# Gathering token rows with one float32 one-hot matmul instead of three bf16 ones, in a two-layer MoE trunk

## The chip, the cores and the metric

The kernel runs on one core of one Trainium2 chip. The metric is the time on the device of one execution, in microseconds (us). Three runs of the kernel before took 1240.8, 1241.95 and 1242.02 us, so the median is 1241.95 us. Lower is better.

## The reference, cut to what matters

Two layers work on 256 tokens (`S`) of width 1024 (`D`), all in float32. Each layer is a token mixer with a LayerNorm, and then a mixture of 64 experts with a LayerNorm. The part around the change is the mixture:

```python
top_idx, top_w = route(xf, w_router, router_bias)   # 8 of 64 experts per token
y = routed_experts(xf, top_idx, top_w, ...) + swiglu(xf, ws_gate, ws_up, ws_down)
# routed_experts: rows xf[tok] are gathered by expert, then
#   h = silu(x @ w_gate[e]) * (x @ w_up[e]);  yb = h @ w_down[e]       (width 256)
# and yb * weight is summed back into each token's row
```

## The kernel before, in words

**Everything on one core.** The residual stream `xs` lies in SBUF as two tiles of 128 tokens by 1024 (f32). Each layer has a prologue (projections, attention, LayerNorm, router, shared expert; some 150 us) and then the routed experts: 32 pairs of experts, one after the other. `SLOTS` is 32, so each expert takes at most 32 tokens per pass. A pair is therefore 64 columns, and a block of two pairs is 128. If an expert has more tokens, further rounds run through a branch; they are not run for these inputs.

**One pair on TensorE** is `body` in the second `run`, L583 to L627. The order of its work is written out by hand:

1. gate and up, L596: 32 f32 matmuls of 64 by 512, half of them in each 64-column half of the array, from `xg` (the gathered tokens, transposed) and the pair's weights `GU`;
2. a quarter of the gather for the next block, `gather`, L511 to L520: 12 matmuls into PSUM bank `G`, only in pairs 0 to 29;
3. `combine` of the pair before (L542);
4. two transposes of the hidden activations (L608), after `h_rd`;
5. another quarter of the gather, only in pairs 0 to 29;
6. down, L622: 64 matmuls, after `hT_sb`;
7. `turn_sel` for the next pair, L522 to L534, in pairs 0 to 30: the one-hot matrix is transposed and the routing weights are gathered into slots.

**The gather.** `sel` is the one-hot matrix (token by slot) that VectorE builds at L1146. `xsp` holds x as three bf16 parts, `hi`, `mid` and `lo`. For each of the 8 slices of 128 features and both token tiles, three matmuls with stationary `xsp[:, t, s, k::KD]` and moving `sel` accumulate in PSUM. ScalarE copies each full bank of G to `xg` (`g_quarter`, L925, recorded at L912). The two blocks take turns on `xT` and `xg_odd`. The first block of a layer is gathered in one go before pair 0: 48 matmuls into four banks, followed by four copies on ScalarE; the gate of pair 0 waits for the last copy (`g_sb`).

**What the parts cost elsewhere.** ScalarE makes `hi` and `mid` (`split`, L1025), VectorE makes the remainder and `lo` (L1109, L1113), and `weights` (L1115 to L1129) splits the routing weights the same way into `w3`. `take_selT` (L1150) copies the transposed one-hot matrix out of G and adds three parts of a weight (L1156).

**The weights' loads.** SyncE (SP) issues every DMA, all on one queue. There are three weight slots in SBUF. SP's `body` (L428) waits until the gate of pair n-3 is done (`h_full`), issues the 4 MB gate and up load of pair n (L411), waits for the down product of pair n-3 (`y_full`) and issues the 2 MB down load of pair n (L414). TensorE waits for `w_in[0]` before the gate and for `w_in[1]` before the down product. Pairs 0 and 1 are loaded during the prologue; that of pair 2 is issued when `sh1` and `acc3` are full, near the prologue's end, and that of pair 3 when the gate of pair 0 is done. After the last pair of the first layer, the attention loads of the next layer follow in the same queue.

In step 2 and step 5 the calls are:

```python
if filling:
    if j == 0:
        pe.wait_ge(ps.sel_rd, first_block + B + 2)
    pe.wait_ge(ps.selT_sb, n + 1)
    gather(ps, first_block + B + 1, 2 * j, (B + 1) % 2)
...
if filling:
    pe.wait_ge(ps.g_sb, fills + 1)
    gather(ps, first_block + B + 1, 2 * j + 1, (B + 1) % 2)
```

Of the kernel before, what the change touches and what calls it, by code (L numbers as in the profile page):

```python
# [25 lines left out]
P = 128  # L26
# [15 lines left out]
SMALL_W = KD * E + E + 2 * HD + 2  # L42
SCRATCH = 9920
BLOCKS = PAIRS // 2
# [98 lines left out]
def build(nc, x, xt, memt, dense, shared_dn, small_w, ln1_g, ln1_b, w_gu, w_dn, ln2_g, ln2_b,  # L143
          consts, before_ones, pool_mat, out):
    with ExitStack() as ctx:
        def sb(name, shape, dt=F32):
            return ctx.enter_context(nc.sbuf_tensor(name, shape, dt))

        def sem(name):
            return ctx.enter_context(nc.semaphore(name))  # L150
# [11 lines left out]
        small = sb("small", [P, 76])  # L162
        identb = sb("identb", [P, P], BF16)
        bo = sb("bo", [P, P])
# [5 lines left out]
        def part(n, dt=F32):  # L170

            v = scratch[:, off[0]:off[0] + n]
            off[0] += n
            assert off[0] <= SCRATCH, off[0]
            return v if dt == F32 else v.bitcast(dt)
# [20 lines left out]
        off[0] = 0  # L196
        xsp = part(NT * 3 * D // 2, BF16).rearrange("p (t s d) -> p t s d", t=NT, s=3)
        xres = part(NT * D).rearrange("p (t d) -> p t d", t=NT)
        yres = xres[:, 0, :]
        off[0] -= D  # L200
        xg_odd = part(KD * 2 * P)
# [3 lines left out]
        sg = part(2 * F).rearrange("p (t n) -> p t n", t=NT)  # L205
        sel = part(2 * NT * P // 2, BF16).rearrange("p (b t c) -> p b t c", b=2, t=NT)
        selT = part(2 * P // 2, BF16).rearrange("p (b s) -> p b s", b=2)
        pos = part(NT * E)
        w3 = part(NT * E * 3 // 2, BF16).rearrange("p (t e s) -> p t e s", t=NT, s=3)

        off[0] = NT * 3 * D // 2 + D + KD * 2 * P
        sig = part(NT * E)
        biased = part(NT * E)
        masked = part(NT * E)
        chosen = part(NT * E)
        wts = part(NT * E)
        wres = part(NT * E)
        chosenb = part(NT * E // 2, BF16)
# [6 lines left out]
        top = part(NT * 8)  # L225
        assert off[0] <= NT * 3 * D // 2 + D + KD * 2 * P + 3 * D // 2
        counts_i = sb("counts_i", [P, 1], I32)
# [16 lines left out]
        def cc(name):  # L244
            return cst[:, CONSTS[name][0]:CONSTS[name][1]]
# [23 lines left out]
        x_in = sem("x_in")  # L269
        setup_done = sem("setup_done")  # L270
        small_in = sem("small_in")
# [15 lines left out]
        route_rd = sem("route_rd")  # L287
        w3_rd = sem("w3_rd")
        split_hi = sem("split_hi")
        split_rs = sem("split_rs")  # L290
        split_rd = sem("split_rd")
        ssilu = sem("ssilu")
# [35 lines left out]
        def x_at(l, i, t):  # L328

            return x_ready, 4 * l + 2 * i + t + 2  # L330
# [166 lines left out]
        def _(pe):  # L497
# [13 lines left out]
            def gather(ps, B, quarter, buf, to=G):  # L511

                for kk in range(2):
                    k = 2 * quarter + kk
                    for t in range(NT):
                        for s in range(3):
                            m = pe.matmul(to[:].rearrange("p (k x t c) -> p k x t c", k=2, x=4, t=NT)[:, kk, :, t, :],  # L517
                                          xsp[:, t, s, k::KD], sel[:, buf, t, :].rearrange("p (x c) -> p x c", x=4),
                                          start=s == 0, stop=s == 2)
                m.then_inc(ps.g_full, 1)  # L520

            def turn_sel(ps, q):  # L522

                if ps is not main:
                    stand_alone(pe)
                gb = G[:].bitcast(BF16)
                half = sel[:, q // 2 % 2, :, 64 * (q % 2):64 * (q % 2) + 64]
                for t in range(NT):
                    pe.transpose(gb[64 * t:64 * t + 64, 0:P], half[:, t, :], identb[:])  # L529
                for t in range(NT):  # L530
                    wq = w3[:, t].rearrange("p (r e) s -> p r (e s)", e=2)
                    m = pe.matmul(G[64 * t:64 * t + 64, 256:262], half[:, t, :], wq[:, q, :],
                                  start=True, stop=True)
                m.then_inc(ps.selT_ps, 1)  # L534
# [36 lines left out]
            def run(ps, l, turn, round_):  # L571
# [7 lines left out]
                if round_ is None:  # L579
                    pe.wait_ge(w3_rd, l + 1)  # L580
                turn_sel(ps, 0)
# [55 lines left out]
            for l in range(DEPTH):  # L637
# [172 lines left out]
                if l == 0:  # L810
                    pe.wait_ge(setup_done, 1)
                turn_probs(0)
# [89 lines left out]
                shared_down(l)  # L902
                pe.wait_ge(split_rd, 2 * l + 2)
                run(main, l, l, None)
# [4 lines left out]
        def _(act):  # L909

            def copy(out_, in_, **kw):
                return act.activation(out_, in_, ACT.Copy, **kw)  # L912
# [44 lines left out]
            for l in range(DEPTH):  # L957
# [66 lines left out]

                def split(t, part):  # L1025

                    if part == 0:
                        act.wait_ge(*x_at(l, 0, t))
                        copy(xsp[:, t, 0, :], xs[:, t, :]).then_inc(split_hi, 1)
                    else:  # L1030
                        act.wait_ge(split_rs, 2 * l + t + 1)
                        copy(xsp[:, t, 1, :], xres[:, t, :]).then_inc(split_hi, 1)

                def turned_tile(t):
# [13 lines left out]
                turned_tile(0)  # L1048
                split(0, 0)
                exp_logits(0)  # L1050
                turned_tile(1)
                split(1, 0)
                exp_logits(1)
                prepare(ACT.Silu)
                split(0, 1)
                shared_silu(0)
                shared_silu(1)
                evac(l, "shT", hT)
                split(1, 1)
                run(main, l, l, None)  # L1060
# [4 lines left out]
        def _(dve):  # L1065
            dve.memset(small[:], 0.0)
            dve.memset(power[:], -0.5).then_inc(power_set, 1)
            for s_ in [*read, x_ready]:
                dve.sem_inc(s_, 1)
            dve.wait_ge(const_in, 32)  # L1070
            dve.tensor_copy(identb[:], ident).then_inc(setup_done, 1)
            links = [0]
# [33 lines left out]

            def split_residual(l, t):
                dve.wait_ge(split_hi, 4 * l + t + 1)
                dve.tensor_tensor(xres[:, t, :], xs[:, t, :], xsp[:, t, 0, :], ALU.subtract).then_inc(split_rs, 1)  # L1109

            def split_last(l, t):
                dve.wait_ge(split_hi, 4 * l + 2 + t + 1)
                dve.tensor_tensor(xsp[:, t, 2, :], xres[:, t, :], xsp[:, t, 1, :], ALU.subtract).then_inc(split_rd, 1)  # L1113

            def weights(l, t):  # L1115

                def tile(v, n=E):
                    return v[:, t * n:(t + 1) * n]
                chosen_, sig_, wts_, wres_ = map(tile, (chosen, sig, wts, wres))
                link(dve.tensor_tensor_reduce(wts_, chosen_, sig_, 1.0, 0.0, ALU.mult, ALU.add, wsum[:, t:t + 1]))  # L1120
                link(dve.reciprocal(wrec[:, t:t + 1], wsum[:, t:t + 1]))
                link(dve.tensor_scalar(wts_, wts_, wrec[:, t:t + 1], ROUTED_SCALE, ALU.mult, ALU.mult))
                part3 = [w3[:, t, :, s_] for s_ in range(3)]
                link(dve.tensor_copy(part3[0], wts_))
                link(dve.tensor_tensor(wres_, wts_, part3[0], ALU.subtract))
                link(dve.tensor_copy(part3[1], wres_))
                m = dve.tensor_tensor(part3[2], wres_, part3[1], ALU.subtract)
                if t == NT - 1:
                    m.then_inc(w3_rd, 1)  # L1129

# [4 lines left out]
            def run(ps, l, turn, round_):  # L1135
# [14 lines left out]
                def take_selT(n, b):  # L1150
                    dve.wait_ge(ps.selT_ps, n + 1)
                    dve.tensor_copy(selT[:, b, :], G[:].bitcast(BF16)[:, 0:P])
                    for t in range(NT):
                        for e in range(2):
                            r0 = 64 * t + 32 * e
                            m = dve.tensor_reduce(wslot[r0:r0 + 32, b:b + 1], G[r0:r0 + 32, 256 + 3 * e:259 + 3 * e],  # L1156
                                                  AX.X, ALU.add)
                    m.then_inc(ps.selT_sb, 1)
                build_sel(0)
                if round_ is None:  # L1160
                    split_residual(l, 1)
                    split_last(l, 0)
                    split_last(l, 1)
                    weights(l, 0)
                    weights(l, 1)
                    count_slots(l)
# [38 lines left out]
            for l in range(DEPTH):  # L1205
                begin(dve, l, within)
                if l:
# [3 lines left out]
                                    take(l, "xTa3")[:, :].rearrange("p (k s) -> p k s", k=4)).then_inc(read[BANK_OF["xTa3"]], 1)  # L1211

                cos2 = cc("cos").unsqueeze(1).to_broadcast([P, 2, S])
                sin2 = cc("sin").unsqueeze(1).to_broadcast([P, 2, S])
# [70 lines left out]
                normalised(l, 0, 0)  # L1285
                split_residual(l, 0)

# [113 lines left out]
```

## Time and profile before

| | |
|---|---|
| median of 3 runs | 1241.95 us |
| the profiled execution's own time | 1242.17 us |
| its span, first to last instruction | 1240.2 us |
| mean granted TensorE clock | 0.995 of full speed |
| TensorE matmul busy | 1199.5 us (97% of the span) |
| TensorE weight loads busy | 550.5 us (44%) |
| VectorE / ScalarE busy | 426.9 us / 335.4 us |
| read from HBM | 450.15 MB |

How to read it: PE is TensorE's matmuls, PEld its weight loads (they overlap PE), DVE is VectorE, ACT is ScalarE, SPq is the queue of SyncE, L517 is line 517 of the kernel. Matmuls are pipelined, so the duration of one is longer than the distance between two, and a busy PE is not PE at its peak. The span is about 2 us shorter than the execution's own time. "Landing" is the time from the issue of a DMA to its completion.

### The profile page before, as it was taken

To read this page: it belongs to the slowest core of one execution; us is meant where nothing else is said; L and a number is where in the kernel's file an instruction comes from. 1 tells how busy PE (TensorE), PEld (TensorE's weight loads), DVE (VectorE), ACT (ScalarE), POOL (GpSimd) and SP (SyncE) were. 2 spreads that over 40 slices of the span, in tenths; PEclk is the share of its full clock that TensorE was granted. 3 is DMA by queue.
4 is the path that set the end of the run, shared out by engine and by line. 5 is a ranking of instruction groups with operands and counts; after the bars stand their busy time and mean duration, and the time that the engine had idled before them with its cause. 6 is when DMAs were issued, how large, how long until landed. Compare 5 with 4: busy or idle time off the path is not lost.

```text
span 1240.2 us, 18632 instructions
## 1 busy us (share of the span) xinstructions
PE 1199.5 (97%) x8032; PEld 550.5 (44%) x8032; DVE 426.9 (34%) x1198; ACT 335.4 (27%) x637; POOL 10.4 (1%) x20
## 2 busy tenths in 40 slices
PE   7999899999999999999899999999999999999994
PEld 5764443333443334433386645344333443334431
DVE  0433732332333323333334336233333333333335
ACT  0132222322223222233212323222232222322221
POOL 0000000000000000000010000000000000000001
PEclk9999999999999999999999999999999999999998
DMA  9962389999999999999967405899999999999990
GB/s 390 417 282 80 103 358 435 424 435 425 432 424 427 429 432 429 432 426 433 423 248 309 193 35 221 362 429 430 430 433 427 431 429 428 429 429 428 429 400 37
DMA packets 26713, 452.48 MB, mean 365 GB/s; under 512 B 2944, under 2 KB 3072, under 8 KB 5504
## 3 DMA queue, kind: packets, MB, share of 16 engines
q1 hardware_dynamic: 26624, 451.21, 86.1%
q8 instruction: 66, 1.08, 0.4%
q14 instruction: 23, 0.19, 0.0%
HBM read 450.15 MB, written 1.05 MB: 364 GB/s over the span
## 4 chain that ended last, share of the span: by engine, by line
PE 95%; DVE 3%; DMA 1%; ACT 1%; issue 0%; POOL 0%; SPq 0%; POOLq 0%
PE bank L596 36%; PE bank L622 18%; PE bank L517 8%; PE bank L542 7%; PE bank L678 4%; PE bank L750 4%; PE bank L687 2%; PE bank L608 2%; PE bank L877 1%; PE bank L697 1%; PE bank L566 1%; PE bank L707 1%; PE bank L652 1%; PE bank L646 1%; PE bank L529 1%; DMA slots<-in_dense 1%
## 5 line engine op out<-in xcount | busy, mean ns | idle before, releaser
L622 PE MATMUL bank<-slots,scratch 128*32 128x512 f32 x2048 | 233.0, 595 | 2.3 <-issue 2.3
L596 PE MATMUL bank<-slots,xT 128*64 128x512 f32 x1024 | 226.1, 594 | 1.0 <-ACT xT L912 1.0
L596 PE MATMUL bank<-slots,scratch 128*64 128x512 f32 x1024 | 226.0, 594 | 0.0
L1183 DVE SCALAR_TENSOR_TENSOR scratch<-bank,small,scratch 128x512 f32<-128x512 f32 x128 | 96.1, 751 | 248.7 <-ACT scratch L912 248.7
L912 ACT ACTIVATE scratch<-bank,small 128x512 bf16<-128x512 f32 x128 | 87.9, 687 | 159.0 <-PE bank L622 159.0
L912 ACT ACTIVATE scratch<-bank 128x512 f32<-128x512 f32 (+2 forms) x122 | 67.0, 562 | 236.0 <-PE bank L517 76.9
L517 PEld LDWEIGHTS bank<-scratch 128*128 128x128 bf16 x1536 | 107.7, 146 | 50.4 <-issue 49.7
L596 PEld LDWEIGHTS bank<-slots,xT 128*64 128x64 f32 x1024 | 69.3, 137 | 130.6 <-issue 129.3
L596 PEld LDWEIGHTS bank<-slots,scratch 128*64 128x64 f32 x1024 | 69.2, 137 | 129.4 <-issue 129.4
L517 PE MATMUL bank<-scratch 128*128 128x128 bf16 x1536 | 117.1, 227 | 0.3
L622 PEld LDWEIGHTS bank<-slots,scratch 128*32 128x32 f32 x2048 | 60.8, 109 | 121.1 <-issue 117.1
L1175 DVE TENSOR_TENSOR scratch<-scratch,bank 128x256 f32<-128x256 f32 x64 | 26.9, 421 | 250.0 <-ACT scratch L934 250.0
L934 ACT ACTIVATE scratch<-bank 128x256 f32<-128x256 f32 x64 | 24.6, 384 | 321.2 <-PE bank L596 321.2
L542 PE MATMUL bank<-scratch 64*128 64x512 bf16 x768 | 94.5, 379 | 5.9 <-DVE scratch L1190 5.9
L912 ACT ACTIVATE scratch<-scratch 128x512 bf16<-128x512 f32 (+1 forms) x132 | 84.2, 638 | 21.5 <-DVE scratch L1183 19.2
L1190 DVE TENSOR_TENSOR scratch<-scratch 128x512 bf16<-128x512 f32 x128 | 82.9, 688 | 2.1
L912 ACT ACTIVATE xT<-bank 128x512 f32<-128x512 f32 x75 | 44.1, 597 | 115.2 <-PE bank L517 80.4
L1177 DVE COPY scratch<-bank 128x256 f32<-128x256 f32 x64 | 27.2, 424 | 113.6 <-PE bank L608 113.6
L750 PE MATMUL bank<-slots,scratch 128*128 128x512 f32 x128 | 58.2, 600 | 0.0
L678 PE MATMUL bank<-xT,slots 128*128 128x256 f32 x256 | 55.7, 379 | 1.1 <-DVE xT L1210 1.1
L542 PEld LDWEIGHTS bank<-scratch 64*128 64x128 bf16 x768 | 32.3, 94 | 45.2 <-DVE scratch L1190 7.8
L678 PEld LDWEIGHTS bank<-xT,slots 128*128 128x128 f32 x256 | 48.6, 190 | 7.8 <-issue 1.3
(125 smaller groups left out, 697.2 us busy)
## 6 DMA issues: line engine op xcount, KB each, us to landing
slots<-in_w_gu SPq DMA_DIRECT2D x64, 4096.0 KB, 22.6
slots<-in_w_dn SPq DMA_DIRECT2D x64, 2048.0 KB, 20.9
slots<-in_dense SPq DMA_DIRECT2D x32, 1024.0 KB, 11.3
r<-in_pool_mat SPq DMA_DIRECT2D x2, 1024.0 KB, 19.7
r<-in_ln_g SPq DMA_DIRECT2D x4, 512.0 KB, 4.5
r<-in_ln_b SPq DMA_DIRECT2D x4, 512.0 KB, 5.9
slots<-in_shared_dn SPq DMA_DIRECT2D x2, 1024.0 KB, 4.9
scratch<-in_memt SPq DMA_DIRECT2D x2, 512.0 KB, 6.8
```

The lines of the kernel that those rows point to most:

```text
L517: m = pe.matmul(to[:].rearrange("p (k x t c) -> p k x t c", k=2, x=4, t=NT)[:, kk, :, t, :], xsp[:, t, s, k::KD], sel[:, buf, t, :].rearra ...
L542: m = pe.matmul(acc[2 * t + half][:, :], selT[64 * t:64 * t + 64, b, :], ysp[64 * t:64 * t + 64, s, half * 512:(half + 1) * 512], start=Fa ...
L596: m = pe.matmul(H[64 * a:64 * a + 64, :], xg[B % 2][:, k, j, a, :], GU[g][:, a, :, k, :], start=k == 0, stop=k == KD - 1)
L608: m = pe.transpose(H[:, kc * P:(kc + 1) * P], hh[:, 0, kc::KF], ident)
L622: m = pe.matmul(Y[half][r0:r0 + 32, :], hT[:, kc * P + 64 * a + 32 * t:kc * P + 64 * a + 32 * t + 32], DN[g][:, a, kc, half * 512:(half + ...
L678: m = pe.matmul(o[:, j * S:(j + 1) * S], W[c][:, k, (2 * (i % 2) + j) * P:(2 * (i % 2) + j + 1) * P], xT[:, k, :], start=k == 0, stop=k == ...
L750: m = pe.matmul(o[:, :], mixT[:, k, t * P:(t + 1) * P], w[:, k, :], start=first, stop=k == KD - 1, skip_group_check=True)
L912: return act.activation(out_, in_, ACT.Copy, **kw)
L1175: dve.tensor_tensor(hh[:, 0, :], sg[:, 0, :], H[:, F:2 * F], ALU.mult).then_inc(ps.h_rd, 1)
L1177: dve.tensor_copy(hT[:, 0:F], H[:, 0:F]).then_inc(ps.hT_sb, 1)
L1183: dve.scalar_tensor_tensor(yres[:, half * 512:(half + 1) * 512], Y[half][:, :], wslot[:, b:b + 1], ysp[:, 0, half * 512:(half + 1) * 512], ...
L1190: dve.tensor_tensor(ysp[:, 2, half * 512:(half + 1) * 512], yres[:, half * 512:(half + 1) * 512], ysp[:, 1, half * 512:(half + 1) * 512], ...
```

## The change

The gather takes f32 `xs` itself as the stationary operand and an f32 `sel` as the moving one, with one matmul where there were three. In `turn_sel` the bf16 transposes become f32 matmuls against the identity, and the routing weights are gathered straight from f32 `wts`, two columns for each tile. The four instructions of `turn_sel` are now ordered by tile. `xsp`, `xres`, `w3`, `identb`, all splits (ScalarE's two copies and VectorE's two subtractions per tile and layer, four instructions per tile in `weights`) and their semaphores go. The scratch is laid out anew, with `yres` and `sel` in places of their own.

```diff
             def gather(ps, B, quarter, buf, to=G):
                 for kk in range(2):
                     k = 2 * quarter + kk
                     for t in range(NT):
-                        for s in range(3):
-                            m = pe.matmul(to[:].rearrange("p (k x t c) -> p k x t c", k=2, x=4, t=NT)[:, kk, :, t, :],
-                                          xsp[:, t, s, k::KD], sel[:, buf, t, :].rearrange("p (x c) -> p x c", x=4),
-                                          start=s == 0, stop=s == 2)
+                        m = pe.matmul(to[:].rearrange("p (k x t c) -> p k x t c", k=2, x=4, t=NT)[:, kk, :, t, :],
+                                      xs[:, t, k::KD], sel[:, buf, t, :].rearrange("p (x c) -> p x c", x=4),
+                                      start=True, stop=True)
                 m.then_inc(ps.g_full, 1)
             def turn_sel(ps, q):
-                gb = G[:].bitcast(BF16)
                 half = sel[:, q // 2 % 2, :, 64 * (q % 2):64 * (q % 2) + 64]
                 for t in range(NT):
-                    pe.transpose(gb[64 * t:64 * t + 64, 0:P], half[:, t, :], identb[:])
-                for t in range(NT):
-                    wq = w3[:, t].rearrange("p (r e) s -> p r (e s)", e=2)
-                    m = pe.matmul(G[64 * t:64 * t + 64, 256:262], half[:, t, :], wq[:, q, :],
+                    pe.matmul(G[64 * t:64 * t + 64, 0:P], half[:, t, :], ident, start=True, stop=True)
+                    m = pe.matmul(G[64 * t:64 * t + 64, 256:258], half[:, t, :], wts[:, t * E + 2 * q:t * E + 2 * q + 2],
                                   start=True, stop=True)
...
                 if round_ is None:
-                    pe.wait_ge(w3_rd, l + 1)
+                    pe.wait_ge(weights_rd, l + 1)
...
                 shared_down(l)
-                pe.wait_ge(split_rd, 2 * l + 2)
                 run(main, l, l, None)
...
                 turned_tile(0)
-                split(0, 0)
                 exp_logits(0)
                 turned_tile(1)
-                split(1, 0)
                 exp_logits(1)
                 prepare(ACT.Silu)
-                split(0, 1)
                 shared_silu(0)
                 shared_silu(1)
                 evac(l, "shT", hT)
-                split(1, 1)
                 run(main, l, l, None)
...
                 def take_selT(n, b):
                     dve.wait_ge(ps.selT_ps, n + 1)
-                    dve.tensor_copy(selT[:, b, :], G[:].bitcast(BF16)[:, 0:P])
+                    dve.tensor_copy(selT[:, b, :], G[:, 0:P])
                     for t in range(NT):
                         for e in range(2):
                             r0 = 64 * t + 32 * e
-                            m = dve.tensor_reduce(wslot[r0:r0 + 32, b:b + 1], G[r0:r0 + 32, 256 + 3 * e:259 + 3 * e],
-                                                  AX.X, ALU.add)
+                            m = dve.tensor_copy(wslot[r0:r0 + 32, b:b + 1], G[r0:r0 + 32, 256 + e:257 + e])
                     m.then_inc(ps.selT_sb, 1)
                 build_sel(0)
                 if round_ is None:
-                    split_residual(l, 1)
-                    split_last(l, 0)
-                    split_last(l, 1)
                     weights(l, 0)
```

## Rows read from the trace of the kernel before

**Rows 1.** The page: engines (1), slices of 31 us (2), chain that ended last (4).
```profile
PE 1199.5 (97%) x8032; PEld 550.5 (44%) x8032; DVE 426.9 (34%) x1198; ACT 335.4 (27%) x637; POOL 10.4 (1%) x20
DMA  9962389999999999999967405899999999999990
PE 95%; DVE 3%; DMA 1%; ACT 1%; issue 0%; POOL 0%; SPq 0%; POOLq 0%
```
**Rows 2.** Timeline of one pair: start, length, engine, line, what [idle before].
```profile
500.92 7.06 PE L596 MATMUL bank<-slots,xT 128*64 128x512 f32 x32
507.91 0.95 PE L517 MATMUL bank<-scratch 128*128 128x128 bf16 x12
508.79 1.47 PE L542 MATMUL bank<-scratch 64*128 64x512 bf16 x12
510.19 0.51 PE L608 MATMUL bank<-cst,scratch 128*128 128x128 f32 x2
510.54 0.90 PE L517 MATMUL bank<-scratch 128*128 128x128 bf16 x12
510.74 0.42 DVE L1177 COPY scratch<-bank 128x256 f32<-128x256 f32 x1 [1.87 <-PE bank L608]
511.36 3.64 PE L622 MATMUL bank<-slots,scratch 128*32 128x512 f32 x32
514.93 0.25 PE L529 MATMUL bank<-identb,scratch 128*64 128x128 bf16 x2
515.04 7.06 PE L596 MATMUL bank<-slots,xT 128*64 128x512 f32 x32
```
**Rows 3.** DMA view, loads issued at 169.90, 183.11, 564.53, 1174.40 us, in that order.
```profile
slots<-in_w_gu SPq DMA_DIRECT2D x1, 4096.0 KB, 13.9
...
slots<-in_w_gu SPq DMA_DIRECT2D x1, 4096.0 KB, 15.1
...
slots<-in_w_gu SPq DMA_DIRECT2D x1, 4096.0 KB, 32.6
...
slots<-in_w_gu SPq DMA_DIRECT2D x1, 4096.0 KB, 32.3
```
**Rows 4.** Two stretches: us, busy by engine, PEclk, DMA share, GB/s.
```profile
183.00:597.00 414.00, 413.44 (x3110) 164.19 (x3112) 131.36 (x349) 119.31 (x204) 0.00 (x0) 1.00 1.00 429
168.00:170.00 2.00, 2.00 (x13) 0.62 (x10) 0.00 (x0) 0.10 (x1) 0.00 (x0) 1.00 0.00 0
```
**Rows 5.** Timeline of TensorE, the gates of pair 31 in both layers.
```profile
598.82 7.06 PE L596 MATMUL bank<-slots,scratch 128*64 128x512 f32 x32
...
1208.69 7.06 PE L596 MATMUL bank<-slots,scratch 128*64 128x512 f32 x32
```
**Rows 6.** Timeline of TensorE in the prologues, f32 matmuls of other widths.
```profile
25.05 21.32 PE L678 MATMUL bank<-xT,slots 128*128 128x256 f32 x98
...
138.33 1.16 PE L859 MATMUL bank<-cst,xs 128*128 128x128 f32 x8 [0.68 <-DVE xs L1105]
...
73.78 0.87 PE L795 MATMUL bank<-scratch 128*64 128x256 f32 x8
```
**Rows 7.** Timeline of the first layer before pair 0, and a pair of copies earlier.
```profile
158.95 3.13 PE L517 MATMUL bank<-scratch 128*128 128x128 bf16 x48
159.90 2.82 ACT L912 ACTIVATE xT<-bank 128x512 f32<-128x512 f32 x4 [5.75 <-PE bank L517]
...
162.77 7.09 PE L596 MATMUL bank<-slots,xT 128*64 128x512 f32 x32 [0.51 <-ACT xT L912]
...
139.08 1.08 ACT L912 ACTIVATE xT<-bank 128x512 f32<-128x512 f32 x2 [8.09 <-PE bank L859]
```
**Rows 8.** Timeline of pair 30, which has no gather.
```profile
594.07 0.50 PE L608 MATMUL bank<-cst,scratch 128*128 128x128 f32 x2
594.61 0.42 DVE L1177 COPY scratch<-bank 128x256 f32<-128x256 f32 x1 [0.98 <-PE bank L608]
595.14 3.64 PE L622 MATMUL bank<-slots,scratch 128*32 128x512 f32 x32 [0.56 <-issue]
```

More of the change, by code:

```diff
@@ L42 @@
 SMALL_W = KD * E + E + 2 * HD + 2
-SCRATCH = 9920
+SCRATCH = 9728
 BLOCKS = PAIRS // 2
@@ L162, in build @@
         small = sb("small", [P, 76])
-        identb = sb("identb", [P, P], BF16)
         bo = sb("bo", [P, P])
@@ L196, in build @@
         off[0] = 0
[L197 to L200, printed above, removed]
+        yres = part(D)
+        sel = part(2 * NT * P).rearrange("p (b t c) -> p b t c", b=2, t=NT)
+        off[0] += 4 * D - D - 2 * NT * P
         xg_odd = part(KD * 2 * P)
@@ L205, in build @@
         sg = part(2 * F).rearrange("p (t n) -> p t n", t=NT)
-        sel = part(2 * NT * P // 2, BF16).rearrange("p (b t c) -> p b t c", b=2, t=NT)
         selT = part(2 * P // 2, BF16).rearrange("p (b s) -> p b s", b=2)
         pos = part(NT * E)
-        w3 = part(NT * E * 3 // 2, BF16).rearrange("p (t e s) -> p t e s", t=NT, s=3)
-        off[0] = NT * 3 * D // 2 + D + KD * 2 * P
+        wts = part(NT * E)
+        off[0] = 4 * D + KD * 2 * P
         sig = part(NT * E)
@@ L215, in build @@
         chosen = part(NT * E)
-        wts = part(NT * E)
-        wres = part(NT * E)
         chosenb = part(NT * E // 2, BF16)
@@ L225, in build @@
         top = part(NT * 8)
-        assert off[0] <= NT * 3 * D // 2 + D + KD * 2 * P + 3 * D // 2
+        assert off[0] <= 4 * D + KD * 2 * P + 3 * D // 2
         counts_i = sb("counts_i", [P, 1], I32)
@@ L269, in build @@
         x_in = sem("x_in")
-        setup_done = sem("setup_done")
         small_in = sem("small_in")
@@ L287, in build @@
         route_rd = sem("route_rd")
[L288 to L291, printed above, removed]
+        weights_rd = sem("weights_rd")
         ssilu = sem("ssilu")
@@ L810, in _ @@
                 if l == 0:
-                    pe.wait_ge(setup_done, 1)
+                    pe.wait_ge(const_in, 32)
                 turn_probs(0)
@@ L1023, in _ @@
                 heads_out(5)
[L1025 to L1032, printed above, removed]
                 def turned_tile(t):
@@ L1069, in _ @@
                 dve.sem_inc(s_, 1)
-            dve.wait_ge(const_in, 32)
-            dve.tensor_copy(identb[:], ident).then_inc(setup_done, 1)
             links = [0]
@@ L1105, in normalised @@
                 dve.scalar_tensor_tensor(v, v, rstd[:, t:t + 1], lnb, ALU.mult, ALU.add).then_inc(x_ready, 1)
[L1107 to L1113, printed above, removed]
             def weights(l, t):
@@ L1118, in tile @@
                     return v[:, t * n:(t + 1) * n]
-                chosen_, sig_, wts_, wres_ = map(tile, (chosen, sig, wts, wres))
+                chosen_, sig_, wts_ = map(tile, (chosen, sig, wts))
                 link(dve.tensor_tensor_reduce(wts_, chosen_, sig_, 1.0, 0.0, ALU.mult, ALU.add, wsum[:, t:t + 1]))
                 link(dve.reciprocal(wrec[:, t:t + 1], wsum[:, t:t + 1]))
[L1122 to L1127, printed above, removed]
+                m = dve.tensor_scalar(wts_, wts_, wrec[:, t:t + 1], ROUTED_SCALE, ALU.mult, ALU.mult)
                 if t == NT - 1:
-                    m.then_inc(w3_rd, 1)
+                    m.then_inc(weights_rd, 1)
             def count_slots(l):
@@ L1211, in _ @@
                                     take(l, "xTa3")[:, :].rearrange("p (k s) -> p k s", k=4)).then_inc(read[BANK_OF["xTa3"]], 1)
+                if l == 0:
+                    dve.wait_ge(const_in, 32)
                 cos2 = cc("cos").unsqueeze(1).to_broadcast([P, 2, S])
@@ L1285, in _ @@
                 normalised(l, 0, 0)
-                split_residual(l, 0)
                 def choose(t):
```

## The prediction

> **What bounds the kernel now.** I read the page first: the chain that ended last is TensorE for 95%, and its matmuls are busy 97% of the span [rows 1]. That alone would make TensorE the bound and every TensorE saving a gain. The DMA row of the slices says otherwise: through both expert stages it stands at 9 in nearly every slice too [rows 1], and the view of stretches gives a DMA share of 1.00 at 429 GB/s from 183 to 597 us [rows 4]. So two resources are full, and the question is which has the slack.
>
> The timeline of one pair gives TensorE's pace: gate to gate 515.04 - 500.92 = 14.12 us, without a gap [rows 2]. The landings give the DMA's. Pair 3's gate load is issued at 169.90 and takes 13.9, so it lands at 183.8; pair 31's is issued at 564.53 and takes 32.6, so it lands at 597.1 [rows 3]. That is 413.3 us for 28 loads, 14.76 us per pair. The DMA is slower than TensorE; each load lands a little later against its issue (15.1 us for pair 4, 32.6 for pair 31), and the stage ends before the head start of three slots is used up. How near it comes: the gate of pair 31 starts at 598.82 [rows 5], 1.7 us after its weights have landed; in the second layer at 1208.69 [rows 5] against 1174.40 + 32.3 = 1206.7 [rows 3], 2.0 us. TensorE is the bound by these 2 us per layer and no more.
>
> **The change, part by part.**
>
> The gather in a pair. Now 12 bf16 matmuls take 507.91 to 508.79 = 0.88 us until the combine starts [rows 2]. Afterwards there are 4 f32 matmuls of 128 columns. No such gather is in the trace; the nearest rows are 98 f32 matmuls of 256 columns in 21.32 us, 0.218 each [rows 6], half of which is 0.11, and eight f32 transposes in 1.16 us [rows 6], 0.14 each with the start and the tail of the group, whose stationary operand is `xs` with the same stride of 8. I take 0.11 each and 0.20 for start and handing over, 0.65 us (0.55 to 0.70). **The first quarter saves 0.23 us** (0.18 to 0.33).
>
> The second quarter lies beside a wait. The down product needs VectorE's copy of the transposed activations: copy at 510.74 for 0.42, down at 511.36 [rows 2]. In pair 30, with no gather between, transposes to down still takes 595.14 - 594.07 = 1.07 us, with the copy [rows 8], against 1.17 with it (511.36 - 510.19, [rows 2]). So **the second quarter saves at most 0.10 us**, I take 0.09: what is late next is the copy. The bounds are 0 and 0.10.
>
> `turn_sel`. Now all four of its instructions hold the next gate up by 515.04 - 514.93 = 0.11 us [rows 2], because they are bf16 and the two column halves overlap. Afterwards each tile has an f32 matmul of 128 columns and one of 2 columns in the same half behind it; ordered by tile, the second tile starts after the first's narrow one. The nearest row is eight f32 matmuls with 64-wide weights in 0.87 us [rows 6], four of them 256 columns wide. I take 0.11 for each tile and 0.08 around, 0.30 us, **0.19 more than now** (0.05 to 0.45 more).
>
> Over one layer 30 pairs have gathers and 31 `turn_sel` calls lie between the gates of pair 0 and pair 31: TensorE's own path gets 30 x 0.32 - 31 x 0.19 = 3.7 us shorter.
>
> The first block of a layer. 48 matmuls take 3.13 us, ScalarE's four copies 2.82 us, and the gate starts at 162.77 after the last copy [rows 7]. With 16 matmuls at 0.11, a bank is full every 0.45 us and the copies become the limit. Two copies in a row take 1.08 us [rows 7], one 0.60, so the step is 0.48 and four take 2.04. A bf16 matmul costs 3.13 / 48 = 0.065 [rows 7], so the first bank is full 0.3 us earlier (12 x 0.065 against 4 x 0.11). Copies from 159.60 to 161.64: **the gate of pair 0 starts 1.1 us earlier** (0.7 to 1.2). The f32 `turn_sel` lies inside that wait.
>
> The splits and the four instructions for `w3`: nothing. VectorE and ScalarE do them under the shared expert's down product and under the shared expert's matmuls; none stands in the chain before the gather, which follows the down product directly. With them gone, that cover hides nothing. `sel` in f32, the copy of `selT` from an f32 bank and four copies for four reductions lie beside a gate of 7.06 us [rows 2]: nothing, and some tenths of a us on VectorE if that cover went. No DMA is added or removed; SP's queue is the same.
>
> What the DMA does with it. Pair 3's load waits for the gate of pair 0, and the DMA is idle then (0 GB/s from 168 to 170 us, [rows 4]), so it moves 1.1 us forward with the gate. After that the queue is never empty and a slot freed earlier only waits longer in it. Pair 31's weights land at 597.1 - 1.1 = 596.0, in the second layer 1206.7 - 1.1 = 1205.6 before the first layer's own gain. TensorE would be ready for them 1.1 + 3.7 = 4.8 us earlier than now, at 594.0. **So it waits there for the load**, some 2 us, and of 4.8 us only 1.7 + 1.1 = 2.8 remain, less 0.1 from landing to first matmul: 2.7 in the first layer, 2.0 + 1.1 - 0.1 = 3.0 in the second.
>
> **The sum:** 1242.17 - 2.7 - 3.0 = 1236.5 us for the profiled execution, which was 0.2 above the median of the runs; for the median 1236.3 us.
>
> Two rules of the Trainium skill bear on this. The landings show a DMA that moves 429 GB/s and not more while it is full [rows 4]. The page "DMA: Bandwidth & Descriptors", section "Where 436 GB/s comes from", puts the ceiling at 435.2 GB/s; a pair's 6.29 MB (4096 + 2048 KB) would take 14.5 us by it, an estimate from that page, which is still slower than TensorE, so the floor would stand. The other rule speaks against the change: f32 at 256 columns costs 0.218 us here [rows 6], two columns' time for each column. "FP8 and Floating Point Precision", section "TensorE Precision Notes", says that true FP32 takes four passes through the array; then four f32 matmuls would cost more than twelve bf16 ones. By that rule, the trace does not agree: it shows half that price.
>
> **The rivals.**
>
> *The DMA gives way (10%).* If the landings could come faster once slots are free earlier, TensorE's whole 4.8 us per layer would count: 1242.0 - 9.6 = 1232.3 us, and with the best bounds of the terms still less. For it: TensorE is the chain's 95%. Against it: a share of 1.00 over 414 us, and landings that fall ever further behind.
>
> *`turn_sel` eats the gather (9%; the other side).* The f32 pieces in `turn_sel` stand open on the path in 31 of 32 pairs. At its upper bound of 0.45 more, with the first quarter at 0.18, TensorE's path grows by 31 x 0.45 - 30 x 0.27 = 5.9 us, less 1.1 at the layer's start: 4.8 us slower per layer, 1251.5 us; at 0.40 and 0.27 it is 1248.5. It decides from 31 x turn - 30 x gather > 1.1 on. Against it: two f32 pieces of 0.11 don't reach 0.4 us.
>
> *Double price per f32 column (2%; the other side).* At 0.22 us for 128 f32 columns, the gather quarter would take 1.07 us instead of 0.88, and the second quarter would outlast its copy. With `turn_sel` at 0.4 more, a pair costs about 0.8 us more and the kernel about 1242 + 2 x (31 x 0.8 - 1) = 1290 us. The row of 256 columns in 0.218 us [rows 6] speaks against it. The rule of four passes, named above, would lead here.
>
> *No change (13%).* The DMA's margin of 2 us could be smaller than it looks, for instance if a wait of 2 us before pair 31 is followed by a stretch of TensorE at 1.2 GHz, or if the loads take 0.3% longer in other runs (1.3 us per layer). Then 1240 to 1243.
>
> **How the numbers follow.** A change under 0.2% (2.5 us) can't be told from none here. The forecast of 1236.3 holds 66%; by its bounds (start 0.7 to 1.2 us, a DMA pace 0.2% off either way) its own range is 1234 to 1239.5. To hold 8 of 10, the range reaches down over most of the first rival and up to no change: 1231.5 to 1242.0. Faster by over 0.2%: the forecast and the first rival, 0.76. Same: no change, 0.13. Slower: the two on the other side, 0.11.
>
> **What the profile afterwards would show.** Right: L517 with 512 f32 matmuls in place of 1536, 0.6 to 0.7 us from gather to combine; the down product 1.1 us after the transposes; about 0.3 us between down and the next gate; the gate of pair 0 of the first layer at 161.7; DMA share 1.00; pair pace near 14.0 us and, in the last one or two pairs, a wait of L596 on DMA of up to 3 us, which doesn't stand in the trace now. Wrong: no wait on DMA at all and the landings closer to their issues (first rival); a pair pace over 14.12 (the other side); an end near 1242 with waits on DMA all over.

## The result: 14% slower, and the profile after

The changed kernel took 1410.8 us (median of 4 runs, 1410.5 to 1411.4) against 1242.0 us before (4 runs of the same comparison). The ratio is 1.136, with a 95% interval of 1.135 to 1.138: 168.8 us slower.

| | before | after |
|---|---|---|
| the profiled execution | 1242.17 us | 1410.57 us |
| its span | 1240.2 us | 1408.7 us |
| PE / PEld busy | 1199.5 / 550.5 us | 1368.4 / 720.7 us |
| DVE / ACT busy | 426.9 / 335.4 us | 417.5 / 327.7 us |
| one pair, gate to gate | 14.12 us | 16.75 us |

The page of the changed kernel: engines, DMA in slices, the chain, and from part 5 the gather's two groups.

```profile
PE 1368.4 (97%) x7776; PEld 720.7 (51%) x7776; DVE 417.5 (30%) x1173; ACT 327.7 (23%) x629; POOL 10.4 (1%) x20
DMA  9941599999999999999747227999999999999930
PE 95%; DVE 2%; DMA 1%; ACT 1%; issue 0%; POOL 0%; SPq 0%; POOLq 0%
L507 PEld LDWEIGHTS bank<-scratch,xs 128*128 128x128 f32 x1024 | 253.0, 332 | 50.7 <-issue 49.2
L507 PE MATMUL bank<-scratch,xs 128*128 128x128 f32 x1024 | 269.0, 407 | 0.9 <-ACT scratch L898 0.9
```

Two things stand in the gather's lines at once. The count is 1024, where I had said 512: the program has 512 f32 matmuls (4 in each quarter), and the profile has two instructions for each. And a weight load takes 332 ns, where the f32 weight loads of the projections take 190. TensorE remains the bound by the same shares as before [rows 1]; the shares say nothing of why it takes longer.

One pair of the changed kernel, TensorE and the copy that the down product waits for (start, length, engine, line, what). It answers to [rows 2]:

```profile
501.34 7.07 PE L583 MATMUL bank<-slots,xT 128*64 128x512 f32 x32
508.34 2.17 PE L507 MATMUL bank<-scratch,xs 128*128 128x128 f32 x8
510.44 1.47 PE L529 MATMUL bank<-scratch 64*128 64x512 bf16 x12
511.84 0.50 PE L595 MATMUL bank<-cst,scratch 128*128 128x128 f32 x2
512.18 2.05 PE L507 MATMUL bank<-scratch,xs 128*128 128x128 f32 x8
512.39 0.42 DVE L1131 COPY scratch<-bank 128x256 f32<-128x256 f32 x1 [3.09 <-PE bank L595]
514.16 3.64 PE L609 MATMUL bank<-slots,scratch 128*32 128x512 f32 x32
517.74 0.45 PE L518 MATMUL bank<-cst,scratch 128*64 128x128 f32 x4
518.09 7.07 PE L583 MATMUL bank<-slots,xT 128*64 128x512 f32 x32
```

The whole difference can be read here. First quarter: 508.34 to 510.44 = 2.10 us for 0.88, so 1.22 more. From transposes to down: 514.16 - 511.84 = 2.32 for 1.17, so 1.15 more; the copy at 512.39 has long been done, and the gather itself now holds up the down product. `turn_sel` to gate: 0.35 for 0.11, so 0.24 more. Together 2.61 us per pair. The pace gives 16.75 - 14.12 = 2.63. Thirty pairs in each of two layers make 158 us.

The start of a layer, which answers to [rows 7] (the first and last copies of four are shown):

```profile
158.72 7.65 PE L507 MATMUL bank<-scratch,xs 128*128 128x128 f32 x32
160.69 0.60 ACT L898 ACTIVATE xT<-bank 128x512 f32<-128x512 f32 x1 [8.99 <-PE bank L507]
...
166.40 0.60 ACT L898 ACTIVATE xT<-bank 128x512 f32<-128x512 f32 x1 [1.31 <-PE bank L507]
167.05 7.09 PE L583 MATMUL bank<-slots,xT 128*64 128x512 f32 x32 [0.25 <-ACT xT L898]
```

The gate of pair 0 starts at 167.05, not at 162.77 [rows 7]: 4.3 us later. In the second layer its distance from the gate of pair 31 before it is 178.4 us for 173.8, 4.5 more; together 8.8. ScalarE's copies wait 1.3 us each for the gather, so they never became the limit. Adding up, 158 + 8.8 + 0.5 (two last calls of `turn_sel`) = 167.3 of the 168.5 us between the spans. The rest stands in the last combine:

```profile
1392.01 2.74 PE L529 MATMUL bank<-scratch 64*128 64x512 bf16 x12 [2.97 <-DVE scratch L1144]
```

It took 2.74 us at a granted clock of 0.50, the level of 1.2 GHz. In the trace of before, the same group, after a wait just as long (2.97 us), took 1.47 us at a clock of 1.00. Nothing in the traces ties this 1.3 us to the change.

### The profile page after: what moved, and what is told of

It is laid out like the page before. It is cut to its first block, busy times and chain, and to the rows that moved or that the text cites. A ratio compares the mean times of both kernels' runs of the same rounds, so it can differ in the third digit from the quotient of the medians.

```text
span 1408.7 us, 18086 instructions
## 1 busy us (share of the span) xinstructions
PE 1368.4 (97%) x7776; PEld 720.7 (51%) x7776; DVE 417.5 (30%) x1173; ACT 327.7 (23%) x629; POOL 10.4 (1%) x20
## 4 chain that ended last, share of the span: by engine, by line
PE 95%; DVE 2%; DMA 1%; ACT 1%; issue 0%; POOL 0%; SPq 0%; POOLq 0%
PE bank L583 31%; PE bank L507 18%; PE bank L609 16%; PE bank L529 7%; PE bank L665 4%; PE bank L737 3%; PE bank L674 2%; PE bank L595 2%; PE bank L518 2%; PE bank L864 1%; PE bank L684 1%; PE bank L553 1%; PE bank L694 1%; PE bank L639 1%; PE bank L633 1%; PE bank L770 1%
## 5 line engine op out<-in xcount | busy, mean ns | idle before, releaser
L507 PEld LDWEIGHTS bank<-scratch,xs 128*128 128x128 f32 x1024 | 253.0, 332 | 50.7 <-issue 49.2
L507 PE MATMUL bank<-scratch,xs 128*128 128x128 f32 x1024 | 269.0, 407 | 0.9 <-ACT scratch L898 0.9
L583 PEld LDWEIGHTS bank<-slots,xT 128*64 128x64 f32 x1024 | 73.8, 137 | 125.8 <-issue 125.1
L583 PEld LDWEIGHTS bank<-slots,scratch 128*64 128x64 f32 x1024 | 74.1, 137 | 124.9 <-issue 124.9
L898 ACT ACTIVATE scratch<-scratch 128x512 bf16<-128x512 f32 x128 | 80.0, 625 | 19.3 <-DVE scratch L1137 19.3
```

What stands on the lines that cost most here:

```text
L583: m = pe.matmul(H[64 * a:64 * a + 64, :], xg[B % 2][:, k, j, a, :], GU[g][:, a, :, k, :], start=k == 0, stop=k == KD - 1)
```

## The experiments

Two facts had to be told apart, the number of passes and the price of one; and the prediction's other half, the floor set by the weights' landings, had not been tested at all, since the changed kernel never came near it.

### The stationary operand's stride: 1, 2, 4 against 8 elements

In each of these three kernels ScalarE copies x once per layer, in the prologue, into `xp`, and the f32 gather takes its stationary operand from there. The result is the same, only the distance between neighbouring stationary elements differs. The lines of the contiguous one, without its semaphore and waits; in the others the 1 is a 2 or a 4:

```diff
+        xp = part(NT * D).rearrange("p (t d) -> p t d", t=NT)
...
-                                      xs[:, t, k::KD], sel[:, buf, t, :].rearrange("p (x c) -> p x c", x=4),
+                                      xp[:, t, k // 1 * 1 * P + k % 1:(k // 1 + 1) * 1 * P:1], sel[:, buf, t, :].rearrange("p (x c) -> p x c", x=4),
...
+                    copy(xp[:, t, :].rearrange("p (g q s) -> p g q s", g=KD // 1, s=1),
+                         xs[:, t, :].rearrange("p (q g s) -> p g q s", g=KD // 1, s=1)).then_inc(xp_rd, 1)
```

Contiguous:

> The changed kernel, but x is copied once per layer into contiguous slices of 128 features, and the f32 gather takes its stationary operand from there. The gather is still 8 f32 instructions per quarter. Theory A (the stationary operand's stride of 32 bytes doubles each weight load): weight loads of the gather fall from 332 ns to about 190, matmuls start 0.11 us apart instead of 0.24, a quarter takes 1.1 us instead of 2.1, a pair 14.75 us instead of 16.75, the kernel about 1285 us. Theory B (an f32 matmul of 128 by 128 costs 0.24 us however its operand lies, because of what f32 adds to a load): no change, about 1410 us. Rival C (the PSUM pattern of the output is what slows it): no change either, 1410 us.

Stride 2:

> As the contiguous copy, but neighbouring stationary elements lie 8 bytes apart (stride 2 in f32). Theory A1 (any stride costs the doubling): weight loads of 332 ns, about 1410 us. Theory A2 (two elements out of each 16 bytes are enough, as the skill's page on cachelines has it): about 190 ns and 1285 us. Theory B: 1410 us.

Stride 4:

> As the contiguous copy, but with stride 4 in f32, 16 bytes apart, one element out of each 16 bytes. Theories A1 and A2 and B: 332 ns and 1410 us. Only if the penalty grows with the distance beyond 16 bytes would it lie between 1285 and 1410 us.

| stride, bytes | weight load, mean | kernel | ratio to before |
|---|---|---|---|
| 4 (contiguous) | 192 ns | 1280.0 us (2 runs) | 1.030 [1.028, 1.032] |
| 8 | 197 ns | 1287.4 us (2 runs) | 1.036 [1.034, 1.038] |
| 16 | 327 ns | 1404.8 us (one run) | 1.131 (one run) |
| 32 (the change) | 332 ns | 1410.8 us (4 runs) | 1.136 [1.135, 1.138] |

The gather's groups by line in the contiguous copy, in the stride of 8 bytes and in that of 16 (busy us, mean ns):

```profile
L509 PEld LDWEIGHTS bank<-scratch 128*128 128x128 f32 x1024 | 124.3, 192 | 50.7 <-issue 49.6 <-ACT scratch L901 1.0
```
```profile
L509 PEld LDWEIGHTS bank<-scratch 128*128 128x128 f32 x1024 | 130.7, 197 | 50.8 <-issue 49.6 <-ACT scratch L901 1.1
```
```profile
L509 PEld LDWEIGHTS bank<-scratch 128*128 128x128 f32 x1024 | 248.4, 327 | 50.7 <-issue 49.2 <-ACT scratch L901 1.3
```

And a pair of the contiguous one:

```profile
508.58 1.16 PE L509 MATMUL bank<-scratch 128*128 128x128 f32 x8
509.67 1.47 PE L531 MATMUL bank<-scratch 64*128 64x512 bf16 x12
511.07 0.50 PE L597 MATMUL bank<-cst,scratch 128*128 128x128 f32 x2
511.41 1.06 PE L509 MATMUL bank<-scratch 128*128 128x128 f32 x8
512.40 3.64 PE L611 MATMUL bank<-slots,scratch 128*32 128x512 f32 x32
```

The quarter falls from 2.10 us to 1.09 (508.58 to 509.67), as theory A had it. B (f32 itself) and C (the output's pattern, which is the same in all four) fall. So does A1: at 8 bytes the load is almost as fast as contiguous, at 16 bytes it is slow, and at 32 hardly slower. That the operand is now in `xp` does not explain it either, since the kernel with 16 bytes reads `xp` too and is slow. The step lies between 8 and 16 bytes, that is between two f32 elements out of 16 bytes and one. The Trainium skill's page "Advanced Engine Details and Errata", section "SBUF Cachelines", describes SBUF as having cachelines of 16 bytes and says that at least two hits on one are needed to absorb the access latency. By that rule, these runs agree. They can't tell it from a rule that goes by the distance alone.

### Load or matmul: half of the moving columns

```diff
-                        m = pe.matmul(to[:]...[:, kk, :, t, :],
+                        m = pe.matmul(to[:]...[:, kk, 0:2, t, :],
-                                      xs[:, t, k::KD], sel[:, buf, t, :].rearrange("p (x c) -> p x c", x=4),
+                                      xs[:, t, k::KD], sel[:, buf, t, :].rearrange("p (x c) -> p x c", x=4)[:, 0:2, :],
```

> The changed kernel with the gather's moving operand cut to 64 of its 128 columns (half of the slots are not gathered). Theory L (the strided weight load is the bound and the matmul hides beside it): the step between matmuls stays 0.24 us and the kernel 1410 us. Theory S (with the stride, load and matmul stand one after the other): the step falls by the time of 64 columns, 0.055 us, to 0.18; a pair is 16 x 0.055 = 0.9 us shorter, the kernel 1355 us. If the matmul itself were slow for its output pattern, the step would halve to 0.12 us and the kernel take 1290.

Half of the slots are not gathered, so this kernel's outputs are wrong and only its times are of use. Measured: 1408.9 us (one run), 1.9 us under the changed kernel. A quarter's gather:

```profile
508.98 1.98 PEld L507 LDWEIGHTS bank<-scratch,xs 128*128 128x128 f32 x8 [0.81 <-issue]
508.98 2.11 PE L507 MATMUL bank<-scratch,xs 128*128 128x64 f32 x8
```

The eight loads still take 1.98 us. In the changed kernel they took 1.98 too. Halving the matmuls' columns changed almost nothing (the group takes 2.11 us for 2.17): the strided load sets the step of 0.24 us, and the matmul hides beside it (theory L).

### `turn_sel` alone in f32

The gather stays as before; VectorE builds a second, f32 one-hot `sel32`, and `wts` has a place of its own.

```diff
-                    pe.transpose(gb[64 * t:64 * t + 64, 0:P], half[:, t, :], identb[:])
-                ...
-                    m = pe.matmul(G[64 * t:64 * t + 64, 256:262], half[:, t, :], wq[:, q, :],
+                    pe.matmul(G[64 * t:64 * t + 64, 0:P], half[:, t, :], ident, start=True, stop=True)
+                    m = pe.matmul(G[64 * t:64 * t + 64, 256:258], half[:, t, :], wts[:, t * E + 2 * q:t * E + 2 * q + 2],
                                   start=True, stop=True)
```

> The kernel before with the gather as it was (three bf16 parts, bf16 one-hot) and only turn_sel in f32, from a second one-hot in f32. Theory A: turn_sel on the path goes from 0.11 to 0.36 us, 0.25 us more for each of 62 calls between gates, 1242 + 15.5 = 1257.5 us. Rival D (what grew in the pair is all in the gather, and turn_sel overlaps the next gate): 1242 us. Rival E (f32 turn_sel costs the 0.19 us of the prediction): 1253.8 us.

Measured: 1260.4 us (median of 4), ratio 1.014 [1.012, 1.016], 18 us more. From one pair to the next in its timeline (other lines left out):

```profile
502.44 0.98 PE L519 MATMUL bank<-scratch 128*128 128x128 bf16 x12
503.36 1.47 PE L541 MATMUL bank<-scratch 64*128 64x512 bf16 x12
509.50 0.45 PE L530 MATMUL bank<-cst,sel 128*64 128x128 f32 x4
509.85 7.07 PE L595 MATMUL bank<-slots,xT 128*64 128x512 f32 x32
516.86 0.98 PE L519 MATMUL bank<-scratch 128*128 128x128 bf16 x12
```

`turn_sel` to gate is 509.85 - 509.50 = 0.35 us, 0.24 more than before. The pair takes 516.86 - 502.44 = 14.42 us, 0.30 more. Of the remaining 0.06 us, 0.04 lies between the first gather and the combine (503.36 - 502.44 = 0.92 for 0.88); why is not shown. Rival D (it overlaps) falls. Theory A gave 15.5 us for the measured 18, rival E 11.8.

**The parts add up.** In medians: `turn_sel` in f32 costs 1260.4 - 1242.1 = 18 us; the f32 gather with a contiguous operand a further 1280.0 - 1260.4 = 20 us, which is what two f32 instructions with 128 columns cost beyond three bf16 ones; the stride of 32 bytes 1410.8 - 1280.0 = 131 us. The stride is nearly four fifths of the loss. Even with a contiguous operand, the f32 gather and `turn_sel` cost 38 us more than the bf16 parts.

### The floor of the landings: fewer bf16 parts

To find out what a faster TensorE would have gained, the gather of the kernel before was cut to one part (x rounded to bf16 for the experts) and to two (x rounded to some 16 bits).

```diff
-                        for s in range(3):
+                        for s in range(1):      (range(2) in the other)
-                                          start=s == 0, stop=s == 2)
+                                          start=s == 0, stop=s == 0)      (stop=s == 1)
```

With two parts, the third is not made (`split_last` is gone), and TensorE waits for `split_hi` in place of `split_rd`.

> The kernel before with only the first bf16 part of x gathered: 4 matmuls per quarter instead of 12 (x is then rounded to bf16 for the experts; the other two parts are made but not gathered). It takes 0.48 us from the first quarter and 0.10 from the second, so TensorE's own path is some 18 us per layer shorter. Floor theory (the weights' landings bound the end, as in the prediction): gain of 2.7 + 3.0 us, 1236.4 us, a wait of TensorE on w_gu in about the last fifteen pairs of a layer, landings 14.76 us apart. Rival (TensorE alone bounds, the DMA can go faster): 1206 us. Rival (early waits make TensorE's clock fall): above 1242 us.

> The kernel before with two bf16 parts of x gathered instead of three (x is then rounded to some 16 bits of mantissa for the experts), and the third part not made. 8 matmuls per quarter: 0.24 us less in the first and 0.09 in the second. Floor theory: the same 1236.4 us as with one part, since 0.33 us per pair already exceeds what the landings allow. Rival (TensorE alone bounds): 1242 - 2 x (30 x 0.33 + 0.8) = 1220.6 us.

Measured: 1232.9 us with one part (4 runs, ratio 0.993 [0.992, 0.995]) and 1232.8 us with two (6 runs, 0.993 [0.992, 0.995]). One part saves 8 matmuls per quarter and two parts 4, and the end is the same. The waits of the one with two parts, and its gates of pairs 27, 29 and 31 in the first layer:

```profile
PE bank L596 <- DMA slots<-in_w_gu: 6.1, 8, 1.3
```
```profile
535.72 7.09 PE L596 MATMUL bank<-slots,scratch 128*64 128x512 f32 x32 [0.62 <-DMA slots<-in_w_gu]
564.93 7.09 PE L596 MATMUL bank<-slots,xT 128*64 128x512 f32 x32 [0.58 <-DMA slots<-in_w_gu]
594.16 7.09 PE L596 MATMUL bank<-slots,scratch 128*64 128x512 f32 x32 [1.26 <-DMA slots<-in_w_gu]
```

Gates of alternate pairs stand 29.2 us apart, 14.6 each, and wait for `w_gu`: that is the DMA's pace. The gates between them wait as long for their loads, but the view puts that down to "issue" (5.4 us in 8 gates). With one part, 12.4 us of waits in 12 gates stand under `w_gu` and 10.8 us in 11 under "issue", and the kernel is no faster. So the floor holds. It lies lower than I put it: 1232.8, not 1236.4 us. In the profiles of two parts and of before, the gate of pair 31 starts at 594.16 against 598.82 [rows 5], 4.7 us earlier where I had 2.7. Pair 3's load, the first after the DMA's pause, in the kernel with two parts:

```profile
168.40 0.33 SPq L411 DMA_DIRECT2D slots<-in_w_gu  x1
```
```profile
slots<-in_w_gu SPq DMA_DIRECT2D x1, 4096.0 KB, 12.2
```

It is issued 1.5 us earlier than before (168.40 for 169.90), not 1.1, and lands 3.2 us earlier (180.6 for 183.8), as it takes 12.2 us and not 13.9 [rows 3]. But only the 1.5 us last. The landings of `w_gu` in the first layer, issue plus time to landing:

| pair | before | two parts | earlier by |
|---|---|---|---|
| 3 | 183.8 | 180.6 | 3.2 |
| 4 | 198.2 | 196.6 | 1.6 |
| 21 | 448.1 | 446.5 | 1.6 |
| 22 | 464.2 | 461.1 | 3.1 |
| 23 | 478.8 | 477.3 | 1.5 |
| 30 | 581.0 | 579.6 | 1.4 |
| 31 | 597.1 | 594.1 | 3.0 |

Landings follow each other after some 14.6 us, but now and then after some 16: before, into pairs 13, 22 and 31, with two parts into 13 and 23. So pair 31 had such a long step before and has none here, and that is the other 1.5 us. What makes a step long is not shown.

In the second layer the gate of pair 31 is 10.5 us earlier (1198.22 for 1208.69), 5.8 us more. 3.2 of them lie between the layer's first and last gate and 1.5 in its first block. The other 1.1 come from TensorE's clock between the layers: after the combine's wait of 2.97 us, which stands in both traces, the granted clock was 0.63 from 616.90 to 620.00 in the trace of before and 1.00 at the same place (612.30 to 616.00) with two parts. The next 32 matmuls took 8.36 us there and 7.17 here.

The kernel with one part has such a stretch among its pairs. Two gates of its trace, one in each layer, and 3.4 us of the second one:

```profile
491.60 7.09 PE L596 MATMUL bank<-slots,xT 128*64 128x512 f32 x32 [2.16 <-issue]
```
```profile
1111.91 8.78 PE L596 MATMUL bank<-slots,xT 128*64 128x512 f32 x32 [2.02 <-DMA slots<-in_w_gu]
```
```profile
1112.20:1115.60 3.40, 3.40 (x10) 0.98 (x8) 1.07 (x2) 0.00 (x0) 0.00 (x0) 0.52 1.02 439
```

The granted clock was 0.52 in this stretch, the lower level of 1.2 GHz, after TensorE had waited 2.02 us, and the gate took 8.78 us instead of 7.09. After the wait of 2.16 us at 491.60 it was 1.00, and the gate took 7.09. So a wait of 2 us can cost another 1.7 us, and its length alone does not say whether it will.

### bf16 parts in contiguous slices

If 16 bytes matter for f32, the bf16 gather of the kernel before, whose stationary elements lie 16 bytes apart, should gain as well. ScalarE and VectorE write the parts in slices instead:

```diff
-                                          xsp[:, t, s, k::KD], sel[:, buf, t, :].rearrange("p (x c) -> p x c", x=4),
+                                          xsp[:, t, s, k * P:(k + 1) * P], sel[:, buf, t, :].rearrange("p (x c) -> p x c", x=4),
...
-                        copy(xsp[:, t, 0, :], xs[:, t, :]).then_inc(split_hi, 1)
+                        copy(xsp[:, t, 0, :].rearrange("p (g q) -> p g q", g=KD), xs[:, t, :].rearrange("p (q g) -> p g q", g=KD)).then_inc(split_hi, 1)
```

The subtraction of `split_residual` is rearranged in the same way.

> The kernel before with the bf16 parts of x stored in contiguous slices of 128 features, so that the gather's stationary elements are 2 bytes apart instead of 16. If the line of 16 bytes matters for bf16 too: weight loads fall from 146 ns to about 94, the step between matmuls from 0.060 to 0.056 us at most (128 columns), 0.05 us less per quarter, up to the floor: 1237 to 1240 us. If bf16 loads are hidden anyway: 1242 us. If the strided reads and writes of the splits on ScalarE and VectorE come on the path: some us above 1242.

Measured: 1239.9 us (12 runs), ratio 0.998 [0.997, 0.999]. Its gather's weight loads and one pair:

```profile
L517 PEld LDWEIGHTS bank<-scratch 128*128 128x128 bf16 x1536 | 91.4, 98 | 50.9 <-issue 49.8 <-ACT scratch L912 0.4
```
```profile
503.31 0.84 PE L517 MATMUL bank<-scratch 128*128 128x128 bf16 x12
504.08 1.47 PE L542 MATMUL bank<-scratch 64*128 64x512 bf16 x12
510.26 7.06 PE L596 MATMUL bank<-slots,xT 128*64 128x512 f32 x32
517.26 0.84 PE L517 MATMUL bank<-scratch 128*128 128x128 bf16 x12
```

The load falls from 146 to 98 ns and the quarter from 0.88 to 0.77 us; the pair takes 517.26 - 503.31 = 13.95 us. That is 0.17 us less in each of 60 pairs, 10 us on TensorE's own path, of which 2.2 us arrive. Two of its gates show what takes the rest:

```profile
582.38 8.78 PE L596 MATMUL bank<-slots,scratch 128*64 128x512 f32 x32 [2.01 <-issue]
```
```profile
1205.04 7.09 PE L596 MATMUL bank<-slots,scratch 128*64 128x512 f32 x32 [2.53 <-DMA slots<-in_w_gu]
```

The first, of pair 30, waits for a load too: its weights landed at 582.3, after a long step. The granted clock was then 0.50 from 582.40 to 585.80, and the gate took 1.7 us longer; after the wait of 2.53 us in the second layer it was 1.00. This run comes nearest to what I had predicted for the change, some 5 us per layer less for TensorE and a wait at the end. The gate of pair 0 starts 0.4 us earlier (162.37), pair 31's weights land 0.4 us earlier (596.7 for 597.1), and its gate starts at 597.23, 1.6 us earlier. By the prediction's sum it would be 1.7 + 0.4 - 0.1 = 2.0. So the floor has no fixed height: it moves with the start of pair 3's load, with the pair that a long step falls on, and with the clock.

It is the fastest version here that gathers all three parts. The ones with two parts and with one are faster, and give up the lower bits of x in the experts.

## Why the prediction was wrong, point by point

- **What bounds the kernel.** Right. TensorE bounds it, with the weights' landings close behind. The runs with fewer parts ran into that floor. Their times lie 3.5 us below my 1236.3. "1.1 us forward" was 1.5 in the run with two parts; the long step that falls on pair 31 before, and in my margins of 1.7 and 2.0, did not fall there; and the clock between the layers gave 1.1. With contiguous bf16 slices, where the start moved by 0.4 us, pair 31's landing in the first layer moved by 0.4 too.
- **The gather in a pair. This step failed, in both of its factors, and it decides the result.** "Afterwards there are 4 f32 matmuls" should have been 8 instructions: each f32 matmul is two. "0.11 each" should have been 0.24. I had 0.65 us for a quarter, and it took 2.10. I had taken the price from f32 rows counted in instructions [rows 6] and multiplied it by a count of matmuls in the program. The rows I had held the factor of two: the program writes 16 gate matmuls per pair and 16 for down, and [rows 2] show x32 for each. My description of the kernel, with 32 and 64 matmuls, is wrong in the same way. For the stride, I had leaned on the eight transposes, whose operand lies the same way, and took their 0.14 us as free of any penalty. The groups of weight loads of the kernel before show it in the same mode, contiguous first, then stride 8:

```profile
L783 PEld LDWEIGHTS bank<-cst,scratch 128*128 128x128 f32 x80 | 9.2, 141 | 4.1 <-issue 3.8
L859 PEld LDWEIGHTS bank<-cst,xs 128*128 128x128 f32 x32 | 3.9, 194 | 7.7 <-DVE xs L1105 7.7
```

  A transpose is one instruction and its load 141 or 194 ns; an f32 matmul is two, and each load 192 or 332. So the stride was not free in the transposes either, and a transpose is no model of a matmul's price.
- **The second quarter.** The wait for the copy was real: with two parts and with one, transposes to down takes 1.07 us, as in pair 30 [rows 8], so 0.10 is all that a shorter gather saves there. With a gather of 2 us it is the copy that hides, and instead of 0.09 less the quarter took 1.15 more.
- **`turn_sel`.** 0.19 us more predicted, 0.24 measured, from 0.35 us on the path for the 0.30 I took. A size slightly off.
- **The first block.** 1.1 us earlier predicted, 4.3 us later measured, by the same price and count.
- **The splits at nothing.** Nothing contradicts it: ScalarE and VectorE are 8 and 9 us less busy, and the gather still follows the down product directly (158.72 against 158.95).
- **The rule that spoke against the change.** The Trainium skill's page "FP8 and Floating Point Precision", section "TensorE Precision Notes", says that true FP32 takes four passes through the array. I wrote that the trace showed half that price. The trace agrees with the page: two instructions of 256 columns at 0.218 us are 0.44 us for one matmul, 256 columns four times at 2.4 GHz. What I had called a disagreement was my miscount.
- **The rivals.** The one with a double price per f32 column had the mechanism of the passes, at 2% and 1290 us; the contiguous f32 gather came out at 1280.0. None had the stride. The range left out every case in which a price taken from a row of another form could be wrong by a factor.

## What to carry to other kernels

Before a price per instruction is multiplied, count the same operation in the program and in the profile: an f32 matmul appears twice, a transpose once. Look at the distance between neighbouring elements of an f32 stationary operand: at 8 bytes its load was nearly as fast as contiguous, at 16 bytes and more it took 1.7 times as long. A single copy into slices, made in the prologue, took 131 of the 169 us away, though not the price of f32 itself. When two resources stand near full, make one of them much cheaper in a test run: where the time stops falling is a floor, and it can lie some us apart between versions.

## What the runs showed of the hardware that I had not expected

- f32 weight loads of 128 columns: 192 ns at 4 bytes between elements, 197 at 8, 327 at 16, 332 at 32. In bf16, 146 ns at 16 bytes and 98 at 2; distances between were not run.
- With the strided load a matmul of 64 columns has the same step as one of 128, 0.24 us.
- TensorE's granted clock was at half after waits of 2.02 and 2.01 us, which made the gates behind them 1.7 us longer; after waits of 2.16 and 2.53 us it was full. After the same wait of 2.97 us it was full in the trace of before and half in that of the changed kernel.
- With the queue never empty, 4 MB and 2 MB loads landed every 14.6 us per pair, but into every ninth or tenth pair the step was about 16 us (before and with two parts).
